# A scheduled attention trunk on one core: bank empties moved one step, pair sums for the B units, and dense work respread

## The reference

```python
proj = einsum('bsd,de->bse', h, w_in_ab)            # layer 0: A and B
qa, ka, va, qb, kb, vb, ga, gb = split(proj)
ya = diff_attention(qa, ka, va, ...)                # A: 4 heads x 2 maps, all earlier keys, ALiBi
yb = sliding_window_gqa(qb, kb, vb, sinks)          # B: 8 heads, this and the previous chunk of 64, sink
y  = concat([ya * silu(ga), yb * silu(gb)]) @ w_out_ab
...
proj = einsum('bsd,de->bse', h, w_in_c)             # layer 1: C
yc = chunked_relpos_attention(qc, kc, vc, rel_bias) # C: 16 heads, band of 9 chunks, relative bias
y  = (yc * silu(gc)) @ w_out_c
```

## Time and profile before

| what | value |
|---|---|
| median of three runs | 1391.14 us |
| the profiled execution's own time | 1392.36 us |
| its span, first to last instruction | 1390.4 us |
| PE matmul busy | 1234.1 us (89%) |
| DVE busy | 891.2 us (64%) |
| ACT busy | 580.6 us (42%) |
| POOL busy | 389.3 us (28%) |
| mean granted TensorE clock | 0.952 of full |

### The profile page before, as it was taken

How to read it: one execution, slowest core, us unless ns; L and a number is a source line. 1 busy time by engine, 2 the same in 40 slices (tenths; PEclk the granted TensorE clock), 3 DMA queues, 4 the chain that set the end, 5 groups by cost and what they waited for, 6 DMA issues and landing times.

```text
span 1390.4 us, 17337 instructions
## 1 busy us (share of the span) xinstructions
PE 1234.1 (89%) x6480; PEld 1043.0 (75%) x6480; DVE 891.2 (64%) x1789; ACT 580.6 (42%) x1271; POOL 389.3 (28%) x280
## 2 busy tenths in 40 slices
PE   6999999999878877768568999999999999998863
PEld 6978888888766665656457888888888888886652
DVE  5575857677576676765444386766847586675667
ACT  5544434434333434433333444444444354443332
POOL 4322131231423334433722212213230222312002
PEclk9999999999999999889779999999999999999976
DMA  6341020110211122222211111102110211111302
GB/s 197 107 127 61 16 62 16 35 42 16 62 46 46 48 78 91 91 76 61 91 61 46 51 46 50 46 16 65 31 65 16 65 31 50 46 35 31 121 31 91
DMA packets 86243, 82.07 MB, mean 59 GB/s; under 512 B 3184, under 2 KB 74864, under 8 KB 86160
## 3 DMA queue, kind: packets, MB, share of 16 engines
q1 hardware_dynamic: 86160, 80.97, 18.6%
HBM read 72.52 MB, written 13.68 MB: 62 GB/s over the span
## 4 chain that ended last, share of the span: by engine, by line
PE 74%; DVE 13%; ACT 5%; issue 4%; POOL 2%; DMA 1%; SPq 0%; POOLq 0%; DVEq 0%; ACTq 0%
PE dense L926 38%; PE dense L933 13%; PE pv_ps L1004 8%; PE scores L1078 6%; PE turned L1048 5%; PE dense L901 3%; DVE e_sb L1410 2%; DVE y L1387 2%; DVE rec_wide L1449 1%; DVE pT_lo L1474 1%; ACT e_sb L1176 1%; DVE yT_lo L1530 1%; PE dense L960 1%; ACT pT_hi L1205 1%; PE turned L1036 1%
## 5 line engine op out<-in xcount | busy, mean ns | idle before, releaser
L926 PE MATMUL dense<-hT_hi,w_hi 128*128 128x512 f32 x880 | 354.8, 403 | 0.0
L926 PE MATMUL dense<-hT_lo,w_hi 128*128 128x512 f32 x880 | 348.5, 396 | 0.0
L926 PE MATMUL dense<-hT_hi,w_lo 128*128 128x512 f32 x880 | 347.9, 395 | 0.0
L1176 ACT ACTIVATE e_sb<-e_sb,low 128x256 f32<-128x256 f32 (+7 forms) x256 | 170.7, 667 | 371.3 <-DVE low L1410 371.3
L799 POOL TENSOR_SCALAR w_hi<-w_f 128x1024 fp32r<-128x1024 f32 x90 | 102.0, 1133 | 793.2 <-PE dense L926 663.7
L802 POOL TENSOR_TENSOR w_lo<-w_f,w_hi 128x1024 fp32r<-128x1024 f32 x90 | 219.7, 2441 | 7.5
L926 PEld LDWEIGHTS dense<-hT_hi,w_lo 128*128 128x128 f32 x880 | 167.8, 191 | 37.7
L926 PEld LDWEIGHTS dense<-hT_lo,w_hi 128*128 128x128 f32 x880 | 168.6, 192 | 28.9
L926 PEld LDWEIGHTS dense<-hT_hi,w_hi 128*128 128x128 f32 x880 | 168.4, 191 | 29.2
L1474 DVE TENSOR_TENSOR pT_lo<-turned,pT_hi 128x640 fp32r<-128x640 f32 (+3 forms) x224 | 133.7, 597 | 55.7 <-ACT pT_hi L1205 52.7
L933 PE MATMUL dense<-w_hi,yT_hi 128*128 128x512 f32 x256 | 111.0, 434 | 62.6 <-DVE y L1387 43.6
(11 more groups left out here) (128 smaller groups left out, 1789.5 us busy)
## 6 DMA issues: line engine op xcount, KB each, us to landing
w_f<-in_w_in_c SPq DMA_DIRECT2D x36, 512.0 KB, 4.0
w_f<-in_w_in_ab SPq DMA_DIRECT2D x34, 512.0 KB, 3.9
w_f<-in_w_out_ab SPq DMA_DIRECT2D x12, 512.0 KB, 3.6
rel_tiles_dram<-rel_rows_dram SPq DMA_DIRECT2D x1, 5120.0 KB, 23.1
bias<-rel_tiles_dram SPq DMA_DIRECT2D x8, 640.0 KB, 5.3
y<-in_x SPq DMA_DIRECT2D x8, 512.0 KB, 7.7
xs<-in_x SPq DMA_DIRECT2D x8, 512.0 KB, 3.6
x_dram<-y SPq DMA_DIRECT2D x8, 512.0 KB, 4.1
```

The source lines that it names most:

```text
L926: last = mm(dense[:, x.n % 2, :], lhs[:, d * P:(d + 1) * P], rhs[:, d, x.f * HALF:(x.f + 1) * HALF], start=i == 0, stop=i == 23)
L1176: copy(e, e, ACT.Exp, scale=-1.0, bias=stat_col(low, it.j), accum_out=stat_col(total, it.j)).then_inc(s_exp, 1)
```

## The change

1. **Bank empties one step later.** ACT and DVE drain a finished block in the step after it (`drain`), but in a unit's tail in the same step. DVE does an out that PE issued behind its dense work (`LATE_AT`) in the next step, behind `lowest`, `lo_of_turned`, `normalise` and the denominators of that step; when a step has two bank-2 uses the first (`EARLY_AT`) stands ahead of PE's dense work and is drained in the same step.
2. **Order of a step.** PE now does `turn` and `score` before `turn_rec` and `times_v`. DVE does `lowest` before `lo_of_turned`.
3. **B.** The tile of a deferred item is turned one step earlier, B's `times_v` two steps after the turn instead of one, and `pT_hi`, `pT_lo` hold two pairs of B's tiles (`pT_set`). The outs of B0 and B1 (and so on) go into one bank together: 6 matmuls and one addition in the place of twice 3 and two, so 32 in the place of 64 additions. Their second weight block has a place of its own (slots 4 and 5).
4. **Inverses.** DVE takes the reciprocal of 128x4, ACT `widen` copies it to 128x256.
5. **Dense work respread.** A3's outs over 11 steps, C6's over 16, one a step; blocks of C0, C1 and C7 shifted between steps; C0 gets one step more; the last outputs start a step earlier; the whole program has 2 steps fewer, 320 in the place of 322.
6. The bias of C0 is loaded 10 steps ahead of C0 (before 40) and masked 7 ahead (before 30).

```diff
+    def step(self, j):
+        return self.start + j + (1 if self.kind == "C" and self.i == 0 and j >= 8 else 0)
...
-TOTAL = C[7].start + 30
+TOTAL = C[7].start + 27
...
-            g_ = Turned("p", u_, -1, it_.step + 3, item=it_, first=ITEMS[-2] if u_.kind == "A" else it_)
+            g_ = Turned("p", u_, -1, it_.step + (2 if u_.deferred else 3), item=it_, first=ITEMS[-2] if u_.kind == "A" else it_)
...
-                pv_ = Pv(u_, h_, t_ - 1, len(PVS), g_.step + 1, g_)
+                pv_ = Pv(u_, h_, t_ - 1, len(PVS), g_.step + (2 if u_.kind == "B" else 1), g_)
...
+    f_.tail = any(u_.in_tail(f_.step) and f_.step < u_.step(20) for u_ in UNITS if u_ is not C[7])
+    f_.drain = f_.step if f_.tail else f_.step + 1
...
-for i_ in range(7):
-    s_ = B[i_].start + 13
-    out_steps(B[i_], [(s_, 2), (s_ + 1, 2), (s_ + 2, 2), (s_ + 3, 2)])
+for i_ in range(0, 6, 2):
+    s_ = B[i_ + 1].start + 8
+    out_steps((B[i_], B[i_ + 1]), [(s_ + t, 1) for t in (3, 4, 6, 7, 8, 9, 11, 12)])
...
+EARLY_AT, LATE_AT = {}, {}
+for s_ in range(TOTAL):
+    uses_ = [x for x in SPARES if x.step == s_]
+    EARLY_AT[s_], LATE_AT[s_] = (uses_[:1], uses_[1:]) if len(uses_) > 1 else ([], uses_)
...
     @block.tensor
         for s in range(TOTAL):
...
+            for x in EARLY_AT[s]:
                 spare_use(x)
             project(*PROJ_AT.get(s, (0, 0)))
-            for x in late[:1]:
+            for x in LATE_AT[s]:
                 spare_use(x)
-            for r, _, p in recs_at(s, 4):
-                turn_rec(r, p)
-            for p in PVS_AT[s]:
-                times_v(p)
             for x in TURNED_AT[s]:
                 if x.what == "p":
                     turn(x)
             for it in ITEMS_AT[s]:
                 score(it)
+            for r, p in RECS_AT[s]:
+                turn_rec(r, p)
+            for p in PVS_AT[s]:
+                times_v(p)
...
     @block.scalar
+        def widen(r, it):
...
+            copy(rec_wide[:].rearrange("p (o h a) -> p h o a", o=2, h=2),
+                 stat_col(rec, it.j - 3, 4).rearrange("p (h o a) -> p h o a", h=2, a=1).broadcast_to([P, 2, 2, HD]),
+                 ACT.Copy).then_inc(s_rwide, 1)
...
     @block.vector
-            nc.vector.reciprocal(rec_wide[:].rearrange("p (o h a) -> p h o a", o=2, h=2),
-                                 src.rearrange("p (h o a) -> p h o a", h=2, a=1).broadcast_to([P, 2, 2, HD])).then_inc(s_drec, 1)
+            nc.vector.reciprocal(stat_col(rec, it.j - 3, 4), src).then_inc(s_drec, 1)
...
         for s in range(TOTAL):
+            for it in ITEMS_AT.get(s - 1, []):
+                lowest(it)
             for x in TURNED_AT[s - 1]:
                 lo_of_turned(x)
-            for it in ITEMS_AT.get(s - 1, []):
-                lowest(it)
             for it in ITEMS_AT.get(s - 2, []):
                 if not it.u.deferred:
                     normalise(it)
-            for r, it, _ in recs_at(s, 2):
+            for r, it in DENOMINATORS_AT[s]:
                 denominators(r, it)
...
+            for x in LATE_AT.get(s - 1, []) + EARLY_AT[s]:
+                spare_use(x)
...
-            for x in uses[len(early):]:
-                spare_use(x)
```

More of the change, by code:

```diff
@@ L90 @@
 BRIDGE = 8
-C = [Unit("C", i, 80 + 64 + BRIDGE + 20 * i) for i in range(8)]
+C = [Unit("C", i, 80 + 64 + BRIDGE + 20 * i + min(i, 1)) for i in range(8)]
 UNITS = A + B + C
@@ L163 @@
     hi: int = 0
+    tail: bool = False
+    drain: int = 0
 @dataclass(eq=False)
@@ L170 @@
     use: int
-    u: Unit = None
+    units: tuple = ()
     row: int = 0
     half: int = 0
-    block: object = None
+    blocks: tuple = ()
 @dataclass(eq=False)
@@ L201 @@
         k0_ = {"A": 0, "B": max(0, t_ - 1), "C": max(0, t_ - 4)}[u_.kind]
[L202 removed]
+        it_ = Item(u_, h_, t_, len(ITEMS), u_.step(j_), k0_, t_ + 1 - k0_)
         n_ = it_.n
@@ L338, in out_steps @@
         for row, half in fills[n:n + count]:
-            SPARE_RAW.append((step, "out", u, row, half))
+            SPARE_RAW.append((step, "out", units, row, half))
         n += count
-    assert n == len(fills), (u, n)
+    assert n == len(fills), (units, n)
 def even_plan(first, n, steps):
@@ L430, in freed @@
             return ("pro", PRO_DONE[b], 0)
+    if blocks[n].u is B[1]:
+        return ("spare", SUM_OF[A[3]].use + 1, B[0].start + 1)
+    if blocks[n].u is B[7]:
+        return ("fill", FILL_OF["g", B[7], 1].n + 1, FILL_OF["g", B[7], 1].step)
     return None
@@ L479, in final_rows, with gate_of @@
     return [(n, row) for a, n, row in FINAL if a + lag == s]
+def gate_of(u, row):
+    c = u.col(row)
+    return max(g.n for g in GATES if g.u is u and same_columns(g.cols, slice(c, c + P)))
 def previous_gate(u, cols):
@@ L747, in _ @@
             for w in LOADS_AT.get(s, []):
+                if w.u is B[1] and w.b == "o":
+                    if new(s_low, 64):
+                        sp.wait_ge(s_low, 64)
                 freed_by(w.slot_free)
@@ L1262, in _ @@
                 hi_of_turned(x)
+            for it in ITEMS_AT.get(s - 1, []):
+                exp(it)
+            for x in LATE_AT.get(s - 1, []) + EARLY_AT[s]:
+                if x.what == "turn":
+                    hi_of_rows(x)
+            for x in FILLS_AT[s]:
+                if not x.tail:
+                    hi_of_fill(x)
+            for p in PVS_AT.get(s - 1, []):
+                out_low(p)
             for u in A:
@@ L1317, in _ @@
                 copy(junk[:], y[:, row, :], ACT.Square, accum_out=rowstat[:, 0, row:row + 1]).then_inc(f_sq, 1)
+            for x in FILLS_AT[s]:
+                if x.tail:
+                    hi_of_fill(x)
     @block.vector
```

290 lines of the change are left out of this document (154 added, 136 removed).

## The result

The changed kernel takes **1530.47 us** (median of 4 runs, 1526.68 to 1532.87), the kernel before 1390.82 beside it: ratio 1.100, 95% interval 1.0955 to 1.1045, slower. The forecast was 1495 us in a range of 1430 to 1570.

The account below looks back on a forecast made before the run. A and C were taken as bound by PE's own work, B, the bridge, C0 and C7 by chains between engines. 54 + 81 + 15 - 54 - 5 + 18 = +109 on 1392 is 1501, lowered to 1495 us; range 1430 to 1570.

Parts of the forecast that it names:

- C's stall: Units of C: PE's out waits for DVE's later addition, 1.83 us a full-width step, 16 us a unit, C1 to C5 +81.
- A's stall: A1 to A3: PE's outs wait for DVE's later addition, 18 us a unit taken, +54 in all.
- its clock: PE's clock in A and C: 0.9 in the eight wide steps, 2 us a unit, +18 in all.
- POOL's part: In A, DVE's second product beside POOL's subtraction takes 2 us longer a unit; three such splits would cost some 6 us.
- B: B0 to the start of C0: shorter DVE work and fewer additions give -12, -22 and -12 us by piece.
- The rival that B gives nothing: In B, the row chain and POOL's splits set the pace, so no gain: 1540 us, chance 0.08.
- C0: Dense matmuls move into its empty first steps and the wait on the second half's keys gets a step: -8 us.
- at no cost: In A and C, v, k and q blocks drain a step later, banks wanted eight steps on: 0 us.
- C6 and C7: C6: stalls with less dense cover, +15 us; C7 to the end: -5 us, between -30 and +15.
- The clock rival: PE falls to 1.2 GHz in the stalled steps, 14 us a unit over nine units: about 1605 us, chance 0.12.
- The rival on the other side: B, C0 and C7 give their whole room, 160 us, and stalls are 8 us a unit: 1309 us, chance 0.10.
- The signs named: Changed profile: C unit about 95 us, A 94, middle B 26 to 27, B0 to C0 about 270, `y` waits some 190.

Follow-up runs that it names:

- The series: Changed kernel with DVE's additions moved in its list: head 1312.1 us, behind `lowest` 1358.6, behind `lo_of_turned` 1421.7, behind `normalise` (the change) 1530.5.
- double slots: Undone, with additions first in DVE's list: one set of `pT_hi` and `pT_lo`, B's `times_v` one step after the turn; 1323.76 us.

## Why the prediction was right, step by step

**C's stall: right in kind, place and size.** The full-width step stalls 1.71 us (1.83 predicted). C3's twelve waits for `y` are 14.0 us by the brackets and 15.9 by start to start, where 16 was predicted; a thirteenth, of 0.6, is for `yT_lo`. The series prices the chain's links: 88.8 - 81.1 = 7.7 us a unit for `lo_of_turned`, where 12 steps of 0.73 less 2.7 for narrow items are 6.1, and 97.4 - 88.8 = 8.6 for reciprocal and product, where 12 of 0.85 less 1.0 are 9.2. The unit came out at 96 to 98, not 95. C3 and C5, at a clock of 1.00, are 78.5 + 16.6 + 1.3 = 96.4: the 1.3 is the 0.1 us that the first matmul behind each of 13 waits loses, which the sum had left out. C1, C2 and C4 are 97.8 to 98.1 at 0.98, and the 2 us of the clock that were predicted make up the difference.

**A's stall: right; its clock: the term that failed.** The stalls are 17.7 us by the brackets in A1, 18.9 by start to start, and 18 was taken, POOL's 2 included. POOL's part held: one product a unit took 3.1 us (at 192.72, 298.86 and 404.83), not three, though POOL makes five such subtractions in A1. The sum is right in part by luck: the prediction had six pairs of 2.8 us on the mean, with 0.9 in a wide pair's second step, and the trace has seven waits a unit, never in two steps in a row. But the clock was taken at 2 us a unit everywhere, "0.9 in the eight wide steps". It is 0.98 to 1.00 in C1 to C5 and 0.92 in A1, where it costs up to 8.4 us: 18.9 + 8.4 is 27.3, measured 26.8. In A2 and A3, at 0.90, it is up to 10.6 and 10.0. That is 6 to 9 us more in each of three units, about all of the error of A (+83 against +60). With the addition behind `lo_of_turned` A1's nine waits are 1.6 us at most and the clock was full, so the loss goes with A's long stalls (five of 2.1 to 5.5 us in A1). Their length alone doesn't decide it: behind the same wait of 2.13 us the matmuls run at the lower level in C1 (at 897.44) and at full speed in C3 (at 1093.50). The Trainium skill ("TensorE: Matmul & The Clock Gate", "A second HAM failure mode: psum-queue depth-cycling") describes a clock that oscillates where PE is idle for short times between groups of matmuls; A agrees in part (1.2 GHz from 170.5 to 174.1, 0.92 on the mean), C with stalls of 0.4 to 2.1 us hardly (0.98 in three units, 1.00 in two).

**B: right, somewhat small.** -54.0 against -46. B2 and B3 take 25.1 and 24.1 us, a little under the 26 to 27 forecast, B1 and B4 27.8 and 27.5. The parts have the prices that the runs gave: inverses on ACT 25 us in all, double slots 7 to 12, PE's order 13 to 18, and two of the three pairs between 4 and 19. They don't add to a clean sum, since each was undone with the others in place. The rival that B gives nothing is out. B gave more than it showed: with the addition at the head B0 to C0 is 250.0 us, so 13 us of stall stood in B too.

**C0: wrong in sign.** +6.7 against -8. The prediction took the drain one step later "at no cost", since the banks are wanted eight steps on. That holds at six dense matmuls a step. In C0 the second half's k and q fill both banks in one step, and v wants the bank of k in the very next, 4.4 us of wait; the kernel with the early drain took 7.2 us back. This is the step that failed. It is not all: even with the early drain C0 takes 124.4 us, against 125.1 before, so the gain of 8 did not come either. The kernel before had a wait of its own for these keys, 3.5 us at the score, which is gone; but C0 also has one step more, which the sum did not count, a wait of 2.9 us at 750.14 for which the profile names no releaser, and five waits of `turn` for DVE, 2.6 us together, that it did not have before. PE's waits for `xs` and `hT_lo` there are 21.5 us, 19.4 before, which agrees with a row chain that sets the pace of its start; no run tried it. How much of C0 the extra step costs by itself was not tried.

**C6 and C7: right in sign.** C6 +24.3 against 17: its clock was 0.91, up to (1 - 0.91) x 92.8 = 8.4 us where 2 were taken, which is most of the 7 us more. C7 -11.9 against -5. The waits of `times_v` for `pT_lo` there, 13.7 us before, are gone, and those for `y` have grown from 6.8 to 15.6 us.

**The clock rival** (1605) has a grain of truth in A and C6: with 29 us at most in A1 to A3, 8.4 in C6 and some 6 in C1 to C5 the clock costs up to 43 us, where the sum had 18 and the rival 124 (by its own 14 a unit, 126). **The rival on the other side** (1309) needed 160 us from the thin stages and stalls of 8 us a unit. With the addition at the head the thin stages give 81 us, and 1312 is near its number only because the stalls are all but gone. Its argument that DVE loses over a quarter of its work in B was too high: 207.4 us became 162.0, 22%.

**The signs named.** A unit of C 96 to 98 us (95), of A 100 to 106 (94), B0 to C0 263 (270), a middle unit of B 24 to 28 (26 to 27), waits for `y` 167 us (190). PE between 900 and 1200 us was busy 85%, not 80%: the 44 us in which it stood are the 14.6 us of brackets in each of three units.

```profile
900.00:1200.00 300.00, 256.06 (x1324) 208.98 (x1323) 160.79 (x358) 108.03 (x227) 53.53 (x36) 0.99 0.11 33
```

In the best version (addition at the head, C0's keys early) the same stretch has

```profile
900.00:1200.00 300.00, 296.68 (x1625) 253.12 (x1624) 203.85 (x451) 134.84 (x283) 65.51 (x45) 1.00 0.14 41
```

1625 matmuls in the place of 1324: A and C are bound by PE's own work again.

**Error of the median:** 1530 against 1495. By the table, A 23 us, C0 15, C1 to C6 11, less 15 for B and C7 and 2 at the start: 32, and the 6 us that the prediction took off its own sum of 1501; together 38, of which 2 lie between the profiled execution (1532.87) and the median. So the terms that were too low (clock and C0) are offset in part by gains of B and C7 that were larger than forecast, and to that extent the closeness of the number is luck.

## What to carry to other kernels

Before moving a bank's release in a consumer's in-order list, add up what stands ahead of it there since the producer's last result, and subtract the producer's work up to its next use of that bank; if the difference is positive it is paid in every step, and the cure is the place in the list, not less work. Here one block moved in one list was worth 218 us. Release at the head of the consumer's list, or use the bank last in the producer's, but not both: together they make a new loop. Price the clock stage by stage, and check block by block in how many steps a bank is wanted again before its drain is put off: a distance that holds in the long stages need not hold where blocks are filled faster.

## What the runs showed of the hardware that was not expected

- Stalls of 0.4 to 2.1 us every 3 to 7 us left the clock at 0.98 (C1, C2, C4; C2: PE busy 83.3 of 98.1 us) or 1.00 (C3, C5). Stalls of 1.0 to 5.5 us left 0.92 (A1, 86.6 of 104.5 us), with 1.2 GHz seen for 3.6 us behind a 2.57 us stall. A1 with 7.7 us of waits, none over 1.6, had 1.00.
- The first 512-column matmul behind a wait holds up the next for 0.33 us, not 0.23 (288.81 to 289.14).
- A DVE product with two SBUF inputs takes 2.65 us for 384 columns beside POOL's subtraction, 1.02 us for 768 without it.
- A reciprocal 256 wide costs DVE 1.75 us, one 4 wide 0.18; ACT copies the 4 to 256 columns in 0.40.
